# Spare products of ones by ones on TensorE at the pauses of a two-layer hybrid encoder step

## The reference

```python
h = rmsnorm(x, norm1_g); z = h @ w_in            # split among four head groups
x += concat(MLA(z_a), DiffAttn(z_b), SGU(z_c), GatedDeltaNet(z_d)) @ w_out
a = causal_dwconv(rmsnorm(x, norm2_g) @ w_up)    # width 3
x += (silu(a_gate) * a_up) @ w_down              # 2816 wide
# after two layers: y = rmsnorm(x, final_g); caches and states are returned too
```

## Time and profile before

| | |
|---|---|
| time, median of 3 runs | 3504.95 us (3495.65 to 3506.49) |
| the profiled execution | 3498.78 us, of which its span 3496.9 us |
| mean granted TensorE clock | 0.958 |
| TensorE matmul busy | 3241.5 us, 93% of the span |
| VectorE busy | 2034.4 us, 58% |
| ScalarE, GpSimd busy | 901.9 us (26%), 882.9 us (25%) |
| moved by DMA | 237.42 MB, 68 GB/s on average |

### The profile page before, as it was taken

One profiled execution on the slowest core, in us unless ns is written; L12 is line 12 of the kernel. 1 busy time (PEld: TensorE's weight loads), 2 busy tenths in 40 slices (PEclk: granted clock), 3 DMA queues, 4 the chain that ended last, 5 costly groups with the idle time before them and its releaser, 6 DMA issues. The chain is left out here.

```text
span 3496.9 us, 57285 instructions
## 1 busy us (share of the span) xinstructions
PE 3241.5 (93%) x23900; PEld 3041.1 (87%) x23900; DVE 2034.4 (58%) x3548; ACT 901.9 (26%) x1650; POOL 882.9 (25%) x780
## 2 busy tenths in 40 slices
PE   5999987889999999999989999979899999999996
PEld 4988965779999999999978898648799999999996
DVE  7395554564555565555566854546627655555556
ACT  3244244233211111111233432532331111111112
POOL 2221110213322222222342212002143222222223
PEclk9999998899999999999999999979899999999998
DMA  5632231201111111111155322230011111111112
GB/s 211 196 98 98 83 110 46 78 18 37 41 43 43 43 43 37 46 40 43 35 174 154 98 76 86 96 115 9 29 41 43 43 37 43 43 43 43 43 43 71
DMA packets 124020, 237.42 MB, mean 68 GB/s; under 512 B 34276, under 2 KB 84708, under 8 KB 120360
## 3 DMA queue, kind: packets, MB, share of 16 engines
q1 hardware_dynamic: 123752, 233.65, 20.5%
HBM read 176.70 MB, written 56.54 MB: 67 GB/s over the span
## 5 line engine op out<-in xcount | busy, mean ns | idle before, releaser
L264 PE MATMUL PS<-h_split,w_split 128*128 128x384 f32 x3072 | 1063.7, 346 | 28.6 <-PEq L201 14.6
L266 PE MATMUL PS<-h_split,w_split 128*128 128x384 f32 x3072 | 1043.8, 340 | 0.0
L265 PE MATMUL PS<-h_split,w_split 128*128 128x384 f32 x3072 | 1039.8, 338 | 0.0
L259 POOL TENSOR_TENSOR w_split<-w_full,w_split 128x1024 fp32r<-128x1024 f32 (+1 forms) x194 | 470.6, 2426 | 953.6 <-ACT w_split L251 953.6
L264 PEld LDWEIGHTS PS<-h_split,w_split 128*128 128x128 f32 x3072 | 585.4, 191 | 47.1 <-issue 29.9
L265 PEld LDWEIGHTS PS<-h_split,w_split 128*128 128x128 f32 x3072 | 581.6, 189 | 2.4
L266 PEld LDWEIGHTS PS<-h_split,w_split 128*128 128x128 f32 x3072 | 581.8, 189 | 0.0
L251 ACT CAST w_split<-w_full 128x1024 fp32r<-128x1024 f32 (+1 forms) x194 | 202.0, 1053 | 1306.6 <-PE PS L266 1167.5
L2308 DVE TENSOR_TENSOR x<-x,PS 128x384 f32<-128x384 f32 x528 | 285.7, 552 | 178.4 <-PE PS L266 176.7
L264 PE MATMUL PS<-ffn_act,w_split 128*128 128x384 f32 x1056 | 367.9, 348 | 8.2 <-POOL w_split L259 7.1
L265 PE MATMUL PS<-ffn_act,w_split 128*128 128x384 f32 x1056 | 357.9, 339 | 0.0
(11 more groups left out here) (388 smaller groups left out, 4894.1 us busy)
## 6 DMA issues: line engine op xcount, KB each, us to landing
w_full<-in_w_up SPq DMA_DIRECT2D x88, 512.0 KB, 3.2
w_full<-in_w_down SPq DMA_DIRECT2D x44, 512.0 KB, 3.3
w_full<-in_w_in SPq DMA_DIRECT2D x38, 512.0 KB, 3.3
kq_keep<-split_rows SPq DMA_DIRECT2D x128, 128.0 KB, 2.4
kq_row<-kq_keep SPq DMA_DIRECT2D x32, 512.0 KB, 4.4
x<-x_keep SPq DMA_DIRECT2D x2, 4608.0 KB, 17.1
w_full<-in_w_out SPq DMA_DIRECT2D x16, 512.0 KB, 3.3
gdn_y<-y_keep SPq DMA_DIRECT2D x2, 3456.0 KB, 11.6
```

Source lines behind the costliest of these rows:

```text
L259: pool.tensor_tensor(ws[:, n % SSLOTS, 1, 0:w], wf[:, n % WSLOTS, 0:w], ws[:, n % SSLOTS, 0, 0:w].bitcast(F32), ALU.subtract).then_inc(w_l ...
L264: pe.matmul(out, w_hi, a_hi, start=first, stop=False)
L265: pe.matmul(out, w_hi, a_lo, start=False, stop=False)
L266: return pe.matmul(out, w_lo, a_hi, start=False, stop=last)
```

## The change

`busy_product` gives way to `keep_busy(pe, bank, times)`: 2 x `times` fp32 matmuls of `ones` by `ones`, 128 by 128 each, into a bank of PSUM. Nobody reads the results. It is called at eleven places of the code, which makes thirteen points of a layer, since the head norm runs twice, and 144 products in a layer. The counts are 8 products at the end of `sgu_stage`, `diff_stage`, `expand_stage` and `diff_gdn_stage`, 10 at the end of `mla_stage` and `gdn_mix_stage`, 12 after the first product of `diff_stage`, 10 in a head norm between sums and spreading, 4 at the end of the first head norm and 10 at the end of the second, 10 ahead of the last down step, 36 at the end of the feed-forward stage, which is the layer's turn. Where another engine may still read the bank, a wait stands ahead. Nothing else is moved.

```diff
-        def busy_product(pe, out, w=256):
-            pe.matmul(out[:, 0:w], C("ident"), cst[:, CC["upto"][0]:CC["upto"][0] + w], start=True, stop=True)
+        def keep_busy(pe, bank, times):
+            for _ in range(times):
+                for half in range(2):
+                    pe.matmul(PS[:, bank, half * P:(half + 1) * P], ones[:, :], ones[:, :], start=True, stop=True)
...
@@ sgu_stage, end
+                    keep_busy(pe, 4, 4)
@@ mla_stage, end
+                    pe.wait_ge(lready, NB)
+                    keep_busy(pe, 7, 5)
@@ diff_stage, after the first product, and end
                     pe.matmul(PS[:, 7, 0:BLK], ones[:, :], ss[:, NB - 1, :], start=True, stop=True).then_inc(smr, 1)
+                    keep_busy(pe, 0, 6)
...
+                    pe.wait_ge(fa, DIFF_TILES * NB)
+                    keep_busy(pe, 0, 4)
@@ expand_stage, end
+                    pe.wait_ge(wfreed, 3)
+                    keep_busy(pe, 4, 4)
@@ head_norm_stage, after the sums, and end
+                    keep_busy(pe, 1, 5)
...
+                    keep_busy(pe, 1, 2 if start is not None else 5)
@@ diff_gdn_stage, end
+                    pe.wait_ge(fa, JOIN_TILES * NB)
+                    keep_busy(pe, 6, 4)
@@ gdn_mix_stage, end
+                    keep_busy(pe, 5, 5)
@@ ffn_stages
                             pe.wait_ge(w_lod, FFN_W + n + 1)
+                            if c == LAST:
+                                pe.wait_ge(upf, ups * NB)
+                                keep_busy(pe, 3, 5)
                             pe.wait_ge(alo, 2 * (c + 1))
...
+                    keep_busy(pe, 3, 18)
```

## The result

The changed kernel takes 3517.55 us, median of six runs (3514.17 to 3524.25); the kernel before took 3503.72 in the runs beside it (3495.65 to 3506.49). The ratio is 1.0046, with a 95% interval of 1.0035 to 1.0057: slower by 13.8 us between the medians (15.8 between the means, and the ratio is nearer to that), where +4.5 was forecast. The time lies inside the range, but beyond the 0.3% that the forecast called no change: the band "slower by over 0.3%" had been given 0.24. The two profiled executions differ by 15.5 us of span, and the rest of this document says where these went.

What follows compares the result with a forecast made beforehand. TensorE, busy 93% of the span, was taken to bound the kernel. Losses of 13.0 us less gains of 8.5 gave +4.5, so 3509.5 us was expected, range 3497 to 3521, meant to hold 8 in 10.

Steps and rivals of the forecast that it cites:

- The turn: Layer's end: 36 products take 7.9 us against 4.8 of cover, nothing comes back; loss 6.0 us over both layers.
- Ahead of the last down step: Ten products start after the pause and fill nothing; the real product waits 2.2 us more; loss 4.4 us in all.
- diff_gdn_stage's end: Eight products fill the pause, sgu_stage starts at full clock with nothing late behind; gain 1.6 us a layer.
- sgu_stage's end: Eight products fill the pause and delay nobody, mla_stage starts at full clock; gain 1.6 us a layer.
- diff_stage's end: TensorE's 1.7 us gain is mostly absorbed by its wait for `q_stack`; gain 0.3 a layer, 0.6 in all.
- The norms: Ten products between sums and spreading gain 1.5 us in all; those at the second norm's end covered at full clock.
- the second rival: Spare products meet a low clock in the norms and the delta rule's end; +16, or 3521 us; chance 0.13.
- gdn_mix_stage's end: Ten products at half clock end 1.9 us late, 0.6 returns; net loss 1.3 a layer, 2.6 in all.
- Absorbed elsewhere: Products at mla_stage's and expand_stage's ends and diff_stage's start: other engines' work or waits cover them; 0 each.
- The first rival: Every removed low stretch gives back half its length, whatever the stage; 3501 or 3494 us; chance 0.12.

Runs made afterwards that it cites:

- e1: The changed kernel without the 36 products at the layer's turn; 3511.59 us, ratio 1.0027.
- e11: The kernel before with spare products only at the layer's turn, twenty in place of thirty-six; 3501.3 us, ratio 0.9999.
- e9: Kernel before plus eight products at diff_stage's, diff_gdn_stage's and sgu_stage's ends, ten ahead of the last down step's wait, masks behind the token loop; 3492.23 us, ratio 0.9975.
- e6: The kernel before with eight spare products each at the ends of sgu_stage and diff_gdn_stage only; 3492.6 us, ratio 0.9984.
- e7: e6 with VectorE's wait for the parameters' DMA and its two mask products moved behind the token loop; 3494.67 us, ratio 0.9982.
- e8: The kernel before with only the wait for fa and eight spare products at diff_stage's end; 3503.55 us, ratio 1.0006.
- e4: The changed kernel without the products at the two head norms' ends (4 and 10); 3514.05 us, ratio 1.0034.
- e3: The changed kernel without the ten products at the end of gdn_mix_stage; 3516.13 us, ratio 1.0042.
- e12: e9 with SP's store of dv moved from diff_stage's end to behind the load of kq_row and the next weight tile; 3487.5 us, ratio 0.9947.
- e5: The kernel before with only the eight spare products at the end of sgu_stage; 3497.85 us, ratio 0.9991.
- e10: The kernel before with VectorE's parameter wait and mask products behind the token loop, no spare products; 3499.89 us, ratio 0.9996.

## Why the prediction was right and where it was wrong

The direction of the forecast held and its range too; its size, and with it the 0.7 for "no change that a measurement can tell", did not: +4.5 forecast, +13.8 measured, with an interval clear of 1. That the time stayed in the range owes something to luck, since terms that were off by 3 to 5 us came out on both sides. By the prediction's own steps:

**The turn**: right. 3.0 us a layer forecast (7.9 less 4.8 is 3.1), 3.2 at the barrier, 3.6 from GpSimd's last sum to L631 (8.35 us for 4.79), 3.8 and 4.0 by e1. e11 shows that the overhang is all of it.

**Ahead of the last down step**: the sum right, the working wrong. I had the ten products at full clock (2.2 us), although the low stretch, which I left where it was, lies on them. They took 3.7 for that reason, and the real products behind ran mostly at full clock in exchange: net about 2.2 a layer. "The real product starts 2.2 us after GpSimd's low part" was 3.8 (1728.88 against 1725.10). What the place could be worth lay outside the forecast: e9 shows 1.4 gained with the wait behind the products.

**diff_gdn_stage's end**: the step that failed is "I see nothing late behind them in these stages: their DVE work follows TensorE's". DVE's copy of the token tile stood behind a wait for a DMA and 1.42 us of masks, and was late as soon as TensorE was not (e6, e7). The term was -3.2 in the sum; +0.5 was measured. The row was to be had from the timeline of DVE before, which I had not read there:

```profile
343.04 1.42 DVE L381 TENSOR_TENSOR wsT<-wsT,cst 128x512 f32<-128x512 f32 x2 [12.43 <-DMA sgu_b<-in_sgu_b]
```

I had read who ended TensorE's waits, and there was no wait, since at half clock TensorE was itself as late. In after the first copy comes later still: `sgu_b` lands 4.3 us after its issue against 3.7 before, and TensorE waits 1.5 us at this copy where e6 has 0.8; sgu_stage is 63.7 there and 63.1 in e6's first layer.

**sgu_stage's end**: right, 1.4 a layer against 1.6. The Trainium skill's page "TensorE: Matmul & The Clock Gate", section "HAM oscillation — how this bites in real kernels", counts the cold penalty as throttled time times one half. A stretch of 3.41 us makes 1.7 by it, as an estimate; mla_stage shows 1.3 to 1.5. sgu_stage shows at most 0.3 for the same stretch, so there the measurement departs from the rule: in this kernel about half the stretch was the price where TensorE alone set the stage, and much less where another engine's work was as late.

**diff_stage's end**: wrong for the changed kernel, by the prediction's own sign: "I am wrong if diff_gdn_stage gets shorter by 1.7 us", and it got shorter by 2.0 and 2.4, with a wait for `q_stack` of 0.08 and 0.26 us in place of about 2. That the wait absorbs what TensorE gains is right where the chain keeps its length (e8), and the chain counts from the barrier, as was said. What failed is that I took GpSimd's chain as rigid. Its length depends on what the DMA engines still carry at the barrier, and the change delays that barrier by 0.56 us: the second copy came 1.8 and 2.0 us sooner, and TensorE, at full clock, was 1.5 us sooner. -0.6 forecast, -4.5 measured in this pair of traces; by the means over the five traces of after and e1 to e4 against the six with nothing at diff_stage's end it is -2.1 in the first layer and -1.8 in the second. It is the largest gain of the change, and a by-product.

**The norms**: the gain was sized rightly where it was forecast, and the cost was put at nothing. In before the spreading began at half clock in two of the four norms, and there it is 0.7 us shorter with the fill (e4), as forecast. The products at gdn_mix_stage's end shorten the sums of the second norm by some 1.5 more, of which I had given 0.6, under gdn_mix_stage. The products at the norms' ends were "covered where the clock is full", with 2.9 at the second norm where it is low. In after it was low at all four: ten products in 4.64 us and four in 2.08, +3.1 at the second norm, +0.9 at the first. Their size is that of the second rival (2.9), but not its condition: it had the clock low at the end of the sums, and there the ten products ran at full clock (2.50 us); the clock fell during the spreading behind them.

**gdn_mix_stage's end**: overhang 2.3 us in the first layer and 2.7 in the second (from TensorE's last real product to the barrier 1.9 us became 4.1 and 4.6), forecast 1.9; what was to come back, 0.6, came in the next stage (e3: 1.0). Stage lengths scatter between 146.3 and 149.8 without the products, so +4.6 in one pair of traces is partly chance; the means of filled and unfilled traces differ by 2.5 a layer, of which some 1 to 1.5 returns in the norm.

**Absorbed elsewhere**: expand_stage unchanged (11.75 against 11.72), out_stage unchanged (108.63), diff_stage's start unchanged, as said. The attention behind expand_stage was given 0; the five kernels that fill its pause have 84.6 to 84.9 us in the first layer, the nine that don't 82.3 to 85.6. That is +1.2 and +1.1 in the mean. The stage's length follows the time that the clock is low in it: in the 18 unfilled layers it takes 82.3 to 82.7 us with 10.2 us at half clock (eight layers), 83.7 to 84.0 with 13.7 (three), 83.7 to 84.8 with 17.1 (six) and 85.6 with 20.5 (one); all ten filled layers have 17.1. So more of this stage, not less, ran at half clock in the filled kernels. No run isolated the eight products at expand_stage's end; whether they do it stays open.

The first rival's end lies 16 us below the result: a low stretch that is gone does not give back half its length whatever the stage. The measured time is nearer to the second rival's 3521, which had 0.13, than to my 3509.5. Its costs at gdn_mix_stage's end and at the second norm's end came about in size, its lost gain and the cost between sums and spreading did not.

## What to carry to other kernels

Before you pay for a faster clock, look for the engine that would be late once TensorE is not: where both sides are equally late the profile shows no wait, and one appears as soon as one side gets faster. The order of the late engine's instructions can then be mended for nothing (1.1 to 1.3 us a layer here, at full clock). Spare products belong ahead of the wait that makes the pause, not behind it. Ahead of a barrier they must end before the last other engine does, counted at the half-clock price if the clock may already be down. And when a barrier moves, read what the DMA queues still carry across it.

## What the runs showed of the hardware

A spare product is 0.22 to 0.25 us at full clock (0.223 in a run of 36, 2.50 us for ten in the norms) and 0.46 to 0.52 at half (4.64 us for ten, 2.08 for four, each with the last one's tail).

The same pause does not always bring the clock down. Pauses of 2.4 to 2.9 us were followed by half clock in three of ten cases at one place, those of 2.9 us in seven of eight at another; filled, in none of 38. The pause of 3.55 us ahead of the last down step was followed by it in 21 of 22. So a single trace doesn't tell whether a place is exposed, and stages differ from run to run by a low stretch's worth without any change in the code.

Adding instructions moved the loads of the program itself. In the traces of after and e1 to e4 the load of a block of instructions (16 KB) began 1.5 to 2.5 us behind sgu_stage's barrier, while the parameters were under way, and in all ten layers `sgu_b` took 4.3 to 5.9 us to land. In e6, e7, e8 and e12 it came 5.0 to 5.7 us behind the barrier, and `sgu_b` took 3.7 to 4.0; in before, e5, e10 and e11 it came at 7.3 or later, and `sgu_b` took 3.7 to 3.9. e9 had it 4.2 and 4.9 us behind, with 5.1 and 3.7; its sgu_stage did not suffer (61.96), since its masks no longer stand ahead of the copies. The load and `sgu_b` in the answer on DMA in after, window 337.32 to 337.82:

```profile
q8 instruction: 1, 0.02, 12.0%
...
sgu_b<-in_sgu_b SPq DMA_DIRECT2D x1, 256.0 KB, 4.3
```

Where the landing came latest, TensorE's wait for DVE's first copy grew to 2.0 to 3.0 us, and in four of five such layers half clock followed some 9 us into sgu_stage: 65.7 and 66.7 (e1), 65.8 (e3), 66.4 (e4), in place of 63.6 to 64.2. No run moved the instruction loads alone, so this is an association over ten layers, not a cause shown.
